# One attention-and-feed-forward kernel: memory result grouped by head pair, two weight residues on GpSimd

## What is computed

```python
def _memory_attention(h, mem, g_q, g_kv, w_q, w_kv, w_o):
    B, S, _ = h.shape
    M = mem.shape[1]
    q = (_rmsnorm(h, g_q) @ w_q).reshape(B, S, MEM_HEADS, MEM_HEAD_DIM)
    kv = (_rmsnorm(mem, g_kv) @ w_kv).reshape(B, M, 2, MEM_HEADS, MEM_HEAD_DIM)
    s = jnp.einsum('bshd,bmhd->bhsm', q, kv[:, :, 0]).astype(jnp.float32) * MEM_HEAD_DIM ** -0.5
    pr = jax.nn.softmax(s, axis=-1)
    o = jnp.einsum('bhsm,bmhd->bshd', pr.astype(h.dtype), kv[:, :, 1])
    return o.reshape(B, S, MEM_HEADS * MEM_HEAD_DIM) @ w_o
...
        h = h + _memory_attention(h, mem, norm_mem_q[l], norm_mem_kv[l], w_mem_q[l], w_mem_kv[l], w_mem_o[l])
        h = h + _swiglu(_rmsnorm(h, norm_ffn[l]), w_ffn_in[l], w_ffn_out[l])
```

## Time and profile before

| | |
|---|---|
| median of three runs | 741.66 us (741.47 to 741.72) |
| the profiled execution's own time | 741.69 us |
| its span, first to last instruction | 739.9 us |
| busy: PE, DVE, ACT, POOL | 731.5, 588.6, 387.6, 57.7 us |
| granted TensorE clock | 1.000 |

### The profile page before, as it was taken

The page is one execution under the profiler, slowest core; times in us unless marked ns, Lnnn a source line. Parts: engine busy times, 40 slices in busy tenths (PEclk is TensorE's granted clock), DMA queues, the critical chain, the costliest instruction groups (busy, mean ns, idle before and its releaser), DMA issues.

```text
span 739.9 us, 14937 instructions
## 1 busy us (share of the span) xinstructions
PE 731.5 (99%) x6320; PEld 718.8 (97%) x6320; DVE 588.6 (80%) x849; ACT 387.6 (52%) x542; POOL 57.7 (8%) x61
## 2 busy tenths in 40 slices
PE   8999999999999999999999999999999999999998
PEld 8999998899999999999999999999999999999997
DVE  5757569989987688999998898978878986687554
ACT  6558557875676444344345566456545554334340
POOL 0007102304000000000000000301110000000000
PEclk9999999999999999999999999999999999999999
DMA  9844553445733579999997435564354465678511
GB/s 335 319 148 164 205 187 116 126 160 197 260 115 116 185 266 364 352 335 325 320 329 262 171 105 214 203 220 171 115 202 147 165 228 196 237 263 310 191 58 58
DMA packets 24114, 156.09 MB, mean 211 GB/s; under 512 B 3568, under 2 KB 3696, under 8 KB 6000
## 3 DMA queue, kind: packets, MB, share of 16 engines
q1 hardware_dynamic: 24048, 155.14, 58.9%
HBM read 154.08 MB, written 1.05 MB: 210 GB/s over the span
## 4 chain that ended last, share of the span: by engine, by line
PE 91%; DVE 4%; ACT 1%; issue 1%; DMA 1%; SPq 0%; DVEq 0%
PE bank L819 16%; PE bank L820 16%; PE bank L821 16%; PE bank L902 9%; PE bank L904 9%; PE bank L905 9%; PE bank L827 3%; PE bank L829 3%; PE bank L830 3%; DVE sb_lo L1928 1%; PE bank L1291 1%; PE bank L1352 1%; DMA sb_raw<-in_stream 1%; PE bank L1304 1%; ACT sb_hi L1470 1%
## 5 line engine op out<-in xcount | busy, mean ns | idle before, releaser
L1928 DVE TENSOR_TENSOR sb_lo<-sb_raw,sb_hi 128x2048 fp32r<-128x2048 f32 (+1 forms) x114 | 260.0, 2284 | 76.8 <-ACT sb_hi L1470 76.3
L1470 ACT CAST sb_hi<-sb_raw 128x2048 fp32r<-128x2048 f32 (+1 forms) x114 | 215.8, 1896 | 100.3 <-PE bank L905 48.0
L819 PE MATMUL bank<-sb_u_hi,sb_hi 128*128 128x256 f32 (+1 forms) x688 | 193.1, 281 | 1.0 <-DVE sb_lo L1928 0.9
L820 PE MATMUL bank<-sb_u_lo,sb_hi 128*128 128x256 f32 (+1 forms) x688 | 190.6, 277 | 0.0
L821 PE MATMUL bank<-sb_u_hi,sb_lo 128*128 128x256 f32 (+1 forms) x688 | 190.6, 277 | 0.0
L819 PEld LDWEIGHTS bank<-sb_u_hi,sb_hi 128*128 128x128 f32 (+1 forms) x688 | 128.9, 187 | 4.7 <-issue 4.3
L820 PEld LDWEIGHTS bank<-sb_u_lo,sb_hi 128*128 128x128 f32 (+1 forms) x688 | 129.1, 188 | 0.0
L821 PEld LDWEIGHTS bank<-sb_u_hi,sb_lo 128*128 128x128 f32 (+1 forms) x688 | 129.1, 188 | 0.0
L902 PE MATMUL bank<-sb_hid_hi,sb_hi 128*128 128x256 f32 x432 | 119.3, 276 | 0.0
L904 PE MATMUL bank<-sb_hid_lo,sb_hi 128*128 128x256 f32 x432 | 119.3, 276 | 0.0
L905 PE MATMUL bank<-sb_hid_hi,sb_lo 128*128 128x256 f32 x432 | 119.3, 276 | 0.0
(11 more groups left out here) (374 smaller groups left out, 1331.1 us busy)
## 6 DMA issues: line engine op xcount, KB each, us to landing
sb_raw<-in_stream SPq DMA_DIRECT2D x140, 1024.0 KB, 5.2
sb_raw<-in_stream SPq DMA_DIRECT2D x4, 256.0 KB, 5.9
sb_raw<-in_stream SPq DMA_DIRECT2D x2, 512.0 KB, 8.5
sb_mem_t<-in_mem SPq DMA_DIRECT2D x1, 1024.0 KB, 4.9
out<-sb_h SPq DMA_DIRECT2D x4, 256.0 KB, 2.2
sb_const<-in_constants SPq DMA_DIRECT2D x1, 838.0 KB, 11.5
sb_h<-in_x SPq DMA_DIRECT2D x1, 572.0 KB, 4.0
sb_h<-in_x SPq DMA_DIRECT2D x1, 512.0 KB, 6.2
```

Of the source, the lines that this page charges most:

```text
L819: nc.tensor.matmul(out, a_hi, b_hi, start=(i == 0), stop=False)
L820: nc.tensor.matmul(out, a_hi, b_lo, start=False, stop=False)
L1470: nc.scalar.copy(place(hi, s)[:, 0:n], x[:, 0:n]).then_inc(sem("hi_ready"), 1)
L1928: tt(place(lo, s)[:, 0:n], x[:, 0:n], f32(place(hi, s)[:, 0:n]), ALU.subtract) \
```

## The change

Three things are altered.

1. The memory result is grouped by head pair. `pv_mem(0, u)` makes the value matmuls of head pair 0 for all four units into bank 3, `pv_mem(1, u)` those of head pair 1 into bank 2. `o_mem`, `turn_mem` and their casts go by head pair. PE turns pair 0 in front of the last unit of pair 1.
2. The output product begins with the first pair. `mem_out` part 0 makes the product of pair 0 (the first 128 rows of the weight block) for two banks. Then pair 1 is turned, and part 1 does the third bank's pair 0 and all the rest. The wait for pair 1's turn stands in front of the 19th matmul. The three fillers remain.
3. The residues of `ffn_in 0` and `ffn_in 1` go to POOL (`pool_residue`), which raises `pool_lo`. DVE waits for it with an empty instruction where the table has the residue, and raises `lo_ready`. The round of `ffn_in 1` on ACT moves ahead of the value matmuls. The residue step of `ffn_in 0` moves behind the first part of the product, that of `ffn_in 1` behind the residual. The division's reciprocal and the release of two score banks move on DVE in front of the value matmuls.

```diff
     add("ssq_cols", 2), add("rstd", 2)
     rounds(where["ffn_in", 0])
+    add("pool_residue", where["ffn_in", 0])
     add("mem_v", 0)
     for u in range(12, 16):
         add("scores", u)
@@ -346,15 +347,22 @@
     evac(where["mem_v",])
     for u in range(12, 16):
         add("turn_p", u)
+    rounds(where["ffn_in", 1])
+    add("pool_residue", where["ffn_in", 1])
+    for u in range(12, 16):
+        add("pv_mem", 0, u)
+    add("o_mem", 0)
+    for u in range(12, 15):
+        add("pv_mem", 1, u)
+    add("turn_mem", 0)
+    add("pv_mem", 1, 15)
+    add("o_mem", 1)
+    add("mem_out", where["mem_o",], 0)
+    add("turn_mem", 1)
     split(where["ffn_in", 0])
-    add("pv", 12), add("pv", 13)
-    add("o_mem", 0)
-    add("pv", 14), add("pv", 15)
-    add("o_mem", 1)
-    add("turn_mem", 0), add("turn_mem", 1)
+    add("mem_out", where["mem_o",], 1)
+    residual(1, 3)
     split(where["ffn_in", 1])
-    block("mem_o", ahead=False)
-    residual(1, 3)
...
-GROUP = {"mem": lambda t: 5 + 5 * t, "fox": lambda t: 6 + t}
+GROUP = {"mem": lambda m: 5 + 5 * m, "fox": lambda t: 6 + t}
...
-O_BANK = {5: 3, 10: 0, 6: 2, 7: 3, 8: 2, 9: 3}
+O_BANK = {5: 3, 10: 2, 6: 2, 7: 3, 8: 2, 9: 3}
...
+            def pv_mem(m, u):
+
+                _, t, i = UNITS[u]
+                g = GROUP["mem"](m)
+                if u == 12:
+                    claim(("o", g), O_BANK[g])
+                if m == 0:
+                    if u == 12:
+                        wait_evacuated(pe, ("block", where["mem_v",]))
+                    wait_evacuated(pe, ("turn_p", u))
+                at = HD * (2 * t + i)
+                for kt in range(NT):
+                    p = prob_t_of(u)[:, (m * NT + kt) * P:(m * NT + kt + 1) * P]
+                    last = nc.tensor.matmul(banks[O_BANK[g]][:, at:at + HD], p,
+                                            vm[:, kt, HD * (i + 2 * m):HD * (i + 2 * m) + HD],
+                                            start=(kt == 0), stop=(kt == NT - 1))
+                if m == 1:
+                    last.then_inc(sem("pv_done"), 1)
+                elif u == 15:
+                    last.then_inc(sem("pv_half"), 1)
+
+            def mem_out(s, part):
+                w_hi, w_lo = weights(s)
+                if part == 0:
+                    claim(("mem_o", 0), 0)
+                    wait_evacuated(pe, ("turn_mem", 0))
+                for c, k in ((0, 0), (1, 0)) if part == 0 else ((2, 0), (0, 1), (1, 1), (2, 1), (3, 0), (3, 1)):
+                    if (c, k) == (0, 1):
+                        wait_evacuated(pe, ("turn_mem", 1))
+                    ps = claim(("mem_o", c), c) if k == 0 and c else banks[c]
+                    for m in range(2):
+                        f = slice((2 * c + m) * P, (2 * c + m + 1) * P)
+                        out = ps[:, m * T:m * T + T]
+                        x1, x2 = mem_t_hi[:, k, :], mem_t_lo[:, k, :]
+                        nc.tensor.matmul(out, w_hi[:, k, f], x1, start=(k == m == 0), stop=False,
+                                         skip_group_check=True)
+                        nc.tensor.matmul(out, w_hi[:, k, f], x2, start=False, stop=False, skip_group_check=True)
+                        last = nc.tensor.matmul(out, w_lo[:, k, f], x1, start=False, stop=(k == 1),
+                                                skip_group_check=True)
+                    if k == 1:
+                        fill(last, ("mem_o", c))
+                used_at[s] = (("mem_o", 3),)
+
...
+            def turn_mem(m):
+
+                wait_evacuated(pe, ("o", GROUP["mem"](m)))
+                ps = claim(("turn_mem", m), "turn")
+                for t in range(NT):
+                    last = nc.tensor.transpose(ps[:, t * P:t * P + P], o_mem[:, t, m * P:m * P + P], ident)
+                fill(last, ("turn_mem", m))
...
+            def pool_residue(s):
+
+                pool.wait_ge(sem("hi_ready"), s)
+                nc.gpsimd.tensor_tensor(place(lo, s)[:, :], raw[:, raw_at["split", s] % RAW, :],
+                                        place(hi, s)[:, :].bitcast(F32), ALU.subtract) \
+                    .then_inc(sem("pool_lo"), 1)
...
                 n = KD * width(s) if width(s) != 256 else BLOCK
+                if blocks[s] in (("ffn_in", 0), ("ffn_in", 1)):
+                    dve.wait_ge(sem("pool_lo"), blocks[s][1] + 1)
+                    nc.vector.engine_nop().then_inc(sem("lo_ready"), 1)
+                    return
                 dve.wait_ge(sem("hi_ready"), s)
...
                 if u in (12, 13):
                     ps = wait_filled(dve, ("turn_p", u))
                     free(nc.vector.tensor_copy(prob_t_of(u), ps[:, :]), ("turn_p", u))
+                if u == 13:
+                    for late in (14, 15):
+                        dve.wait_ge(sem("exp_done"), EXP_ORDER[late] + 1)
+                        free(nc.vector.engine_nop(), ("scores", late))
+                    inverse_den(12, 4)
...
+            def o_mem_(m):
+
+                if m == 0:
+                    dve.wait_ge(sem("pv_half"), 1)
+                else:
+                    dve.wait_ge(sem("pv_done"), 20)
+                key = ("o", GROUP["mem"](m))
+                free(tt(o_mem[:, :, m * P:m * P + P].rearrange("p t (i c) -> p t i c", i=2),
+                        banks[lease[key][0]][:, 0:T].rearrange("p (t i c) -> p t i c", t=NT, i=2),
+                        over(rden[:, 12:16, m].rearrange("p (t i) -> p t i", t=NT), HD), ALU.mult), key)
```

More of the change, by code:

```diff
@@ L957, in take @@
                         args = (part[:, 0], part[:, 1], 2 * (j % 2), j == 2, j == 1)
-                    elif kind == "mem_o":
-                        claim((kind, 0), 0)
-                        for t in range(NT):
-                            wait_evacuated(pe, ("turn_mem", t))
-                        args = (mem_t_hi, mem_t_lo, 0, True, True)
                     else:
@@ L1334, in pv @@
             def pv(u):
                 kind, t, i = UNITS[u]
-                keys = NT if kind == "mem" else t + 1
+                keys = t + 1
                 g = GROUP[kind](t)
@@ L1339, in pv @@
                     claim(("o", g), O_BANK[g])
-                if u == 12:
-                    wait_evacuated(pe, ("block", where["mem_v",]))
                 if u == 16:
@@ L1354, in pv @@
                 last.then_inc(sem("pv_done"), 1)
-            def turn_mem(t):
-                wait_evacuated(pe, ("o", GROUP["mem"](t)))
-                ps = claim(("turn_mem", t), "turn")
-                for m in range(2):
-                    last = nc.tensor.transpose(ps[:, m * P:m * P + P], o_mem[:, t, m * P:m * P + P], ident)
-                fill(last, ("turn_mem", t))
+            def turn_mem(m):
[4 more added lines that the diff above has]
+                fill(last, ("turn_mem", m))
             def forget_sum():
@@ L1743, in turn_o, with turn_mem @@
                                      ACT.Copy, scale=(0.5, 0.5, 1.0)[c]).then_inc(sem("turn_hi"), 1)
-            def turn_mem(t):
-                ps = wait_filled(act, ("turn_mem", t))
-                nc.scalar.copy(mem_t_hi[:, 0:2, t * P:t * P + P], ps[:, 0:T].rearrange("p (m n) -> p m n", m=2)) \
-                    .then_inc(sem("turn_hi"), 1)
+            def turn_mem(m):
+                ps = wait_filled(act, ("turn_mem", m))
+                nc.scalar.copy(mem_t_hi[:, m, :], ps[:, 0:T]).then_inc(sem("turn_hi"), 1)
             def turn_mixed(c):
@@ L1879, in norm_p @@
                 ins.then_inc(sem("rden_ready"), 1)
-            run(dict(norm_p=norm_p, rope1=rope1, cmp_hidden=cmp_hidden, rstd=rstd_of, merge=merge, fox_square=head_stat, mix=lambda part, t: head_stat(2 + part + t)))
+            run(dict(norm_p=norm_p, pool_residue=pool_residue, rope1=rope1, cmp_hidden=cmp_hidden, rstd=rstd_of, merge=merge, fox_square=head_stat, mix=lambda part, t: head_stat(2 + part + t)))
         @block.vector
@@ L2117, in turn_o, with turn_mem @@
                          ALU.subtract), key)
-            def turn_mem(t):
-                key, tok = ("turn_mem", t), slice(t * P, t * P + P)
+            def turn_mem(m):
+                key = ("turn_mem", m)
                 ps = wait_turn_hi(key)
-                free(tt(mem_t_lo[:, 0:2, tok], ps[:, 0:T].rearrange("p (m n) -> p m n", m=2),
-                        f32(mem_t_hi[:, 0:2, tok]), ALU.subtract), key)
+                free(tt(mem_t_lo[:, m, :], ps[:, 0:T], f32(mem_t_hi[:, m, :]), ALU.subtract), key)
             def turn_mixed(c):
@@ L2331, in scores_read @@
                     free(nc.vector.engine_nop(), ("scores", u))
-            def o_mem_(t):
-                dve.wait_ge(sem("pv_done"), 18 + 2 * t)
-                r = rden[:, 12:16, :].rearrange("p u s -> p (u s)")
-                if t == 0:
-                    for u in (14, 15):
-                        free(nc.vector.engine_nop(), ("scores", u))
-                    inverse_den(12, 4)
-                key = ("o", GROUP["mem"](t))
```

(3 more changed lines are left out.)

11 lines of the change are left out of this document (3 added, 8 removed).

## The result

The changed kernel takes 751.04 us (median; 747.41 to 751.17) against 741.69 for the kernel before beside it: ratio 1.0104, 95% interval 1.0088 to 1.0120. The forecast was 745.4, range 741.1 to 748.4. The direction and the place were right, the size was not. The profiled execution took 751.04, its span is 749.3: 9.4 us more than before.

The account below looks back on a forecast made before the run. TensorE was taken as the bound, busy 731.5 of 739.9 us. A hold of +4.2 us less 0.4 for regrouping, with nothing for VectorE's lost residues, gave +3.8 on 741.66: 745.4 us, range 741.1 to 748.4.

Parts of the forecast that it names:

- Term 1: First value matmul to feed-forward on TensorE: regrouping by head pair shortens 11.14 us to 10.72, worth 0.4 us.
- Term 2: VectorE loses two residues of 2.28 and 2.29 us; nothing waited on them, so costed at nothing.
- no second collision: GpSimd's second residue lets go near 231, before VectorE's next instruction with two SBUF inputs near 232; clear by 1 us.
- Term 3: GpSimd's first residue, 4.56 us, holds VectorE's memory scale (L2280) by 4.3 us; value matmuls start 4.2 us later.
- rival 1: At the memory scale: GpSimd's residue does not hold the small VectorE tensor_scalar; time within 0.2% of before; chance 0.22.
- the sum: Whole kernel: +4.2 us from the hold less 0.4 from regrouping, +3.8 us, giving about 745.4.
- rival 2: Granted clock falls from 2.4 to 1.2 GHz after TensorE's wait; 0 to 9 us, taken as 3: 748.4; chance 0.13.
- My own sign of being wrong: In the profile after: granted clock below 1.00 around 220, listed among the signs that would show the forecast wrong.
- Rival 3: GpSimd's residue is much slower with fp32r output: at twice the time the delay is 8.8 us, 750; chance 0.03.

Follow-up runs that it names:

- fillers everywhere: Changed kernel plus 16 filler matmuls on TensorE, before the first turned unit of probabilities and each of the three others; 746.24 us against 742.39, ratio 1.0050.
- fillers first: Changed kernel plus 10 filler matmuls on TensorE before the first turned unit of probabilities only; 746.75 us against 743.01 for the kernel before, ratio 1.0047.
- the second set: Changed kernel, unedited, timed again beside the kernel before and single edits on one chip; 749.84 us against 742.93, ratio 1.0082.

## Why the prediction was wrong

- **Term 1, the regrouping, 10.72 us: right.** The profiles with full clock and both residues on GpSimd have 10.72 to 10.85. Its 0.3 to 0.4 us lie below what the times resolve: the best ratios are 0.9991 to 0.9994.
- **Term 2, the residues off VectorE at nothing: right**, and so was "no second collision": the kernel with only the second residue on GpSimd isn't slower.
- **Term 3, the hold: right in place, kind and size.** GpSimd's residue took 4.60 and 4.53 of an extrapolated 4.56, fp32r added nothing, L2280's successor stood 4.3 us longer (forecast 4.3). Taking the row of 24 columns against rival 1 was right. In "fillers everywhere" the change costs 3.85 us, in "fillers first" 3.74; the sum said 3.8. The sum without the clock was right, within intervals of 2.2 to 4.8 us.
- **The step that failed is the granted clock.** The sum of 3.8 us has it at nothing, and rival 2, "nothing at the least, 9 us if the value matmuls and the product all ran so, and I take 3", had chance 0.13. My own sign of being wrong, a granted clock below 1.00 around 220, came true. The fall came in all six profiles with that wait. In the first profile it cost 4.79 us in the stretch and 0.41 in the transposes; in the second as much in the transposes and next to nothing behind them. By the times of the first comparison the changed kernel cost 9.35 us, with fillers 3.74: 5.6 for the clock. In the second set, 6.91 less 3.74 leaves 3.2. The 3 lay between the short and the long outcome, and the range's 748.4 held only the short one.
- **What led there**: the trace of before showed that 1.52 us of waiting doesn't bring the clock down. It showed nothing for 2.3, the wait that I forecast myself, and TensorE's half-idle four us behind it. A wait past the longest that the trace bears out should have had the fall at even odds or more, and the range its upper bound. The Trainium skill (TensorE: Matmul & The Clock Gate, section "HAM oscillation") names a long idle stretch as what brings the clock down. The traces agree with that, here behind waits of 1.95 to 2.49 us, and I gave it too little.
- Rival 1 didn't happen: two columns were held, and only single columns pass. Rival 3 didn't either: 4.60 us is no slower than the extrapolation.

## What to carry to other kernels

Before a long elementwise instruction goes to GpSimd, list the VectorE instructions that will start under it: here a tensor_scalar from SBUF to SBUF of two columns, 0.17 us of work, stood for 4.49. One-column instructions or another place for GpSimd's instruction avoided it, and smaller pieces cut it to 1.17. Where a delay reaches TensorE as one wait longer than any in the old trace, price the granted clock as a term of the sum, not as an afterthought; its cost can exceed the delay's (5.6 us against 3.7 in the first comparison). A few filler matmuls in the wait test that in one run.
